# Windowed attention with keys on the partitions: four heads a step, maxima taken apart, keys projected between two groups of queries

## The reference, cut to what matters

```
q  = rope(h @ w_q)                       # 512 x 16 x 64; k, v: 512 x 2 x 64, shared by 8 heads each
sc = einsum(q, [k of the tile before, k of this tile]) * 64 ** -0.5
sc = where(0 <= query - key < 128, sc, NEG)           # 4 tiles of 128 queries, 128 or 256 keys
mx = maximum(sc.max(-1), sink)
e  = exp(sc - mx)
p  = e / (e.sum(-1) + exp(sink - mx))
return (p @ v) @ w_out                                 # 1024 x 1024
```

## Time and profile before

| | us |
|---|---|
| median of 3 runs (lowest to highest) | 2175.12 (2169.94 to 2177.8) |
| the profiled execution: its own time | 2168.92 |
| its span in the profile | 2167.1 |
| PE busy | 2060.9 (95%) |
| DVE busy | 1450.6 (67%) |
| ACT busy | 976.3 (45%) |
| granted TensorE clock, mean of the run | 0.982 |

### The profile page before, as it was taken

How to read it: one execution, slowest core, us unless ns; L and a number is a source line. 1 busy time by engine, 2 the same in 40 slices (tenths; PEclk the granted TensorE clock), 3 DMA queues, 4 the chain that set the end, 5 groups by cost and what they waited for, 6 DMA issues and landing times.

```text
span 2167.1 us, 29621 instructions
## 1 busy us (share of the span) xinstructions
PE 2060.9 (95%) x9716; PEld 1653.1 (76%) x9716; DVE 1450.6 (67%) x2421; ACT 976.3 (45%) x1625; POOL 11.1 (1%) x25
## 2 busy tenths in 40 slices
PE   5989999997999989999999999999999999999997
PEld 5988888876777667766667788888877777888885
DVE  6885434463899965667765788883377758888633
ACT  3345433452777632546664433333236743333321
POOL 0000000001000000000000000000000000000000
PEclk9999999987999999999999999999999999999999
DMA  4220122321999705420001233223340022332332
GB/s 153 88 69 1 49 92 92 97 78 39 334 354 358 254 30 155 117 59 1 1 1 50 88 97 97 89 95 107 107 126 25 0 78 87 97 97 90 99 105 84
DMA packets 65175, 218.97 MB, mean 101 GB/s; under 512 B 9392, under 2 KB 10544, under 8 KB 64960
## 3 DMA queue, kind: packets, MB, share of 16 engines
q1 hardware_dynamic: 59792, 210.73, 29.3%
q10 hardware_dynamic: 5296, 7.12, 1.3%
HBM read 209.03 MB, written 2.10 MB: 97 GB/s over the span
## 4 chain that ended last, share of the span: by engine, by line
PE 80%; DVE 12%; ACT 3%; issue 3%; DMA 1%; ACTq 1%; DVEq 0%; SPq 0%
PE psum L812 53%; PE psum L1202 5%; PE psum L1375 2%; PE psum L935 2%; DVE sig L2439 2%; PE psum L958 2%; DVE w_lo L2174 2%; PE psum L975 2%; PE psum L1143 1%; PE psum L974 1%; PE psum L1175 1%; PE psum L1185 1%; PE psum L1358 1%; PE psum L1311 1%; PE psum L931 1%
## 5 line engine op out<-in xcount | busy, mean ns | idle before, releaser
L812 PE MATMUL psum<-x_hi,w_hi 128*128 128x512 f32 (+1 forms) x1440 | 514.5, 375 | 17.8 <-DVE x_lo L2208 6.6
L812 PE MATMUL psum<-x_lo,w_hi 128*128 128x512 f32 (+1 forms) x1440 | 514.0, 374 | 0.0
L812 PE MATMUL psum<-x_hi,w_lo 128*128 128x512 f32 (+1 forms) x1440 | 511.2, 372 | 0.0
L2174 DVE TENSOR_TENSOR w_lo<-raw,w_hi 128x1024 fp32r<-128x1024 f32 x243 | 295.8, 1221 | 198.9 <-ACT w_hi L1498 198.3
L1498 ACT ACTIVATE w_hi<-raw 128x1024 fp32r<-128x1024 f32 x243 | 255.1, 1053 | 184.8 <-DMA raw<-stream 184.5
L812 PEld LDWEIGHTS psum<-x_hi,w_hi 128*128 128x128 f32 x1440 | 263.4, 190 | 73.2 <-issue 8.3
L812 PEld LDWEIGHTS psum<-x_lo,w_hi 128*128 128x128 f32 x1440 | 262.6, 190 | 50.1 <-issue 1.0
L812 PEld LDWEIGHTS psum<-x_hi,w_lo 128*128 128x128 f32 x1440 | 262.8, 190 | 48.6
L812 PE MATMUL psum<-hid_hi,w_hi 128*128 128x512 f32 x624 | 244.4, 392 | 3.4 <-DVE hid_lo L3032 2.0
L812 PE MATMUL psum<-hid_lo,w_hi 128*128 128x512 f32 x624 | 244.7, 392 | 0.0
L812 PE MATMUL psum<-hid_hi,w_lo 128*128 128x512 f32 x624 | 244.0, 391 | 0.0
(11 more groups left out here) (537 smaller groups left out, 3188.7 us busy)
## 6 DMA issues: line engine op xcount, KB each, us to landing
raw<-stream SPq DMA_DIRECT2D x251, 512.0 KB, 3.5
raw<-experts SPq DMA_DIRECT2D x70, 512.0 KB, 5.2
raw_more<-experts SPq DMA_DIRECT2D x68, 512.0 KB, 5.4
staged<-staged ACTq DMA_DIRECT2D x84, 64.0 KB, 2.9
resid<-x_fm SPq DMA_DIRECT2D x4, 528.0 KB, 7.3
out_fm<-resid SPq DMA_DIRECT2D x4, 512.0 KB, 2.9
consts<-consts_in SPq DMA_DIRECT2D x1, 1373.0 KB, 14.2
kv_pairs<-kv_even_odd ACTq DMA_DIRECT2D x4, 256.0 KB, 4.0
```

Of the source, the lines that this page charges most:

```text
L812: last = pe.matmul(o, wt[:, slot, k * P:(k + 1) * P], m[part], start=start and p == 0, stop=stop and p == 2, skip_group_check=True)
L2174: dve.tensor_tensor(w_lo[:, slot, :], raw[:, slot, :], w_hi[:, slot, :].bitcast(F32), ALU.subtract)\
```

## The change

- **Order of the stream.** Queries in two groups of four units, q3a and q3b, with k3 and v3 between them: q3a, k3, v3, q3b, wo3. The inputs of keys and values are made two chunks in each of the four rounds of q3a, by one operation of ACT (L2318) and one of DVE (`kv_low`, L3314).
- **Forms.** Each rotated chunk of queries is written twice, as high part (ACT, `window_queries_high`) and low part (DVE, `window_queries_low`, L3339), stacked on the partitions, in `window_q_parts`; the keys likewise (`window_keys_hi_twice`, `window_keys_lo_and_max`). `window_q_and_max` holds the high part of the queries, and in one row below it the negative maximum.
- **Maxima.** 64 products of high parts (L1563), in 32 fills of two tiles each, alternate in the PSUM banks 1 and 3. DVE reads each fill with two operations that add the band and keep the maximum (L3371). Sixteen fills stand between the units of q3b, four behind each; two stand before the first step and fourteen between the steps of the first quad. A quad is four chunks, eight heads. The maxima of a quad are turned (L1574), joined with the sinks, negated by ACT (L2386) and moved into rows by two DMAs of ACT (L2391).
- **Steps.** Two quads of 14 steps each; a step is (query tile, group, own keys or those before) for four heads: three float32r products of 512 columns (L1589 to L1591: stacked score, mask, stacked score with maximum), one exponential of 512 (L2412), and two steps later one float32 product of 512 columns with the values beside ones (L1603). The sums come out of it as a row.
- **Sums.** SP moves them to rows by DMA, DVE adds the sink's term and takes reciprocals of 32 rows in stretches of 384 and 128 columns. They are split, spread over the partitions by two products (L1613), and DVE weighs the outputs. Per quad this comes after its last step; the first quad's lies beside the second quad's steps.
- **Output projection.** The first four units of wo3 take chunks 0 to 3 (the first quad) each, with the second quad's four spreads behind the second unit, and then chunks 4 to 7, one chunk for each of the four units in turn. So all four slots of weights are held until chunk 7. Units 4 to 7 are as before.

```diff
-         ("q3", 8), ("k3", 1), ("v3", 1), ("wo3", 8), ("ffn1_in", 2 * FC), ("ffn1_out", 24)]
+         ("q3a", 4), ("k3", 1), ("v3", 1), ("q3b", 4), ("wo3", 8), ("ffn1_in", 2 * FC), ("ffn1_out", 24)]
...
+            def window_maxima(f):
+                p, g, first = f // W_FILLS, f // 2 % B_G, 2 * (f % 2)
+                pe.wait_ge(qw_ready, 2 * p + g + 1)
+                if f == 0:
+                    pe.wait_ge(kw_hi, 1)
+                if f >= 2:
+                    pe.wait_ge(wmax_read, 2 * f - 2)
+                for t in (first, first + 1):
+                    k0 = P * max(t - 1, 0)
+                    mm = pe.matmul(window_max_bank(f)[:, 2 * P * (t - first):2 * P * (t - first) + P * (t + 1) - k0], window_parts(g, p)[:, window_tile(t)],
+                                   KW1[:, g, k0:P * (t + 1)], start=True, stop=True)
+                mm.then_inc(wmax_done, 1)
...
+            def window_scores(q, i):
+                t, g, back = W_STEPS[i]
+                n, j = N_W * q + i, t - back
+                if i == 0:
+                    pe.wait_ge(qmw_hi, W_FILLS * (q + 1))
+                    pe.wait_ge(wmax_rows[q], 16 * B_G)
+                if n >= 2:
+                    pe.wait_ge(wexp_done, n - 1)
+                s = by_head(window_score_bank(n))
+                pe.matmul(s, KW1[:, g, window_tile(j)], QW[q][g][:, :, window_tile(t)], start=True, stop=False, skip_group_check=True)
+                pe.matmul(s, (BANDW if back else CAUW)[:, :], ID4[:, :, :], start=False, stop=False, skip_group_check=True)
+                pe.matmul(s, KW2[:, g, window_tile(j)], QMW[q][g][:, :, window_tile(t)], start=False, stop=True, skip_group_check=True).then_inc(ws_done, 1)
+            def window_outputs(q, i):
+                t, g, back = W_STEPS[i]
+                n, x = N_W * q + i, 2 * QT * q + 2 * t + g
+                pe.wait_ge(wexp_done, n + 1)
+                first = back == 1 or t == 0
+                if first and x >= 2:
+                    pe.wait_ge(wo_kept, x - 1)
+                pe.matmul(window_out_bank(x), VW[:, t - back, g * HD:g * HD + P], PW[:, n % 4, :], start=first, stop=back == 0, skip_group_check=True)\
+                  .then_inc(wpv_done, 1)
...
+            for c in range(QUAD, 2 * QUAD):
+                n, r = U["q3b"] + c - QUAD, later_result(c)
+                unit(n, n % SLOTS, r, r % PAIRS, T2, x_of(T2))
+                if c == QUAD:
+                    pe.wait_ge(scaled, 12)
+                    turn(r + 1, VFM[:, :], T2)
+                for f in range(W_FILLS * (c - QUAD), W_FILLS * (c - QUAD + 1)):
+                    window_maxima(f)
+            turn_window_maxima(0)
+            for f in range(W_FILLS * QUAD, W_FILLS * QUAD + 2):
+                window_maxima(f)
...
+            for q in range(QUADS):
+                for i in range(N_W):
+                    window_scores(q, i)
+                    if q == 0:
+                        for f in range(W_FILLS * QUAD + 2 + 2 * i, min(W_FILLS * QUAD + 4 + 2 * i, 2 * W_FILLS * QUAD)):
+                            window_maxima(f)
+                        if i == N_W - 3:
+                            turn_window_maxima(1)
+                    elif 7 <= i < 7 + QUAD:
+                        spread_window(i - 7)
+                    if i >= 2:
+                        window_outputs(q, i - 2)
+                    elif q:
+                        window_outputs(q - 1, N_W + i - 2)
...
+            for c in range(LATE):
+                late_window_chunks(c, range(0, QUAD))
+                if c == 1:
+                    for p in range(QUAD, 2 * QUAD):
+                        spread_window(p)
+            for k in range(QUAD, C):
+                for c in range(LATE):
+                    late_window_chunks(c, range(k, k + 1))
...
+            def rope_unit(n, r, e, turn, scale):
+                by_unit(n)
+                stage(r % PAIRS, e, e % EV_SLOTS, T2, back=2, scale=scale)
+                high_weights(n + AHEAD)
+                swap_halves(e, turn, r + 1)
...
+            for c in range(QUAD, 2 * QUAD):
+                low_weights(U["q3b"] + c - QUAD + AHEAD)
+                rope_turned(c + 1, later_result(c), E0["q3b"] + 2 * (c - QUAD), TURN0["q3b"] + c - QUAD)
+                if c > QUAD:
+                    window_queries_low(c - 1)
+                for f in range(W_FILLS * (c - QUAD), W_FILLS * (c - QUAD + 1)):
+                    read_window_maxima(f)
+            sinks_in_maxima(0)
...
-            rotated("q3", U["q3"], 8, lambda c: Q3[:, c, :], COSR[:, :], SINR[:, :], kv_input)
...
-            attention("swa")
-            residual("wo3", T2, "nf_1", "ffn1")
```

569 lines of the change are left out of this document (411 added, 158 removed).

## The result

The changed kernel takes 2189.96 us (median of 5 runs, 2186.97 to 2191.71) against 2175.12: 14.8 us more, ratio 1.0069 (95% interval 1.0053 to 1.0085). The forecast was 2194, slower, with +18.9 us.

What follows compares the result with a forecast made beforehand. PE, busy 2060.9 of 2167.1 us, was taken to set the time. Three stretches, +55.1 - 48.3 + 12.1 = +18.9 us, on the median of 2175.12 gave 2194; range 2176 to 2206.

Steps and rivals of the forecast that it cites:

- stretch 1: From q3a's start to the first attention step: 118.7 us against 63.6, +55.1.
- stretch 2: Attention: 57.0 us against 105.3, -48.3.
- stretch 3: Output projection (wo3): 56.8 us against 44.7, +12.1; bounds +6 to +15.
- The loop: In q3b, fills wait for DVE reads queued behind the rotation; PE idles, next unit runs cold: three loops of 18.3 us.
- first gap: PE's idle time behind the first unit of q3b, waiting for rotation, reads and last fill: 8.8 us.
- the sign: What would show the forecast right: PE idle before L1563 for around 10 us, DVE named, four times in q3b.
- Keys and values: In k3, PE waits 5.0 us for input chunk 6, made late by DVE's rounds in q3a.
- Attention: 28 steps of 0.70 + 0.91 us, with fills, transposes, spreads 1.9, waits and a cold start: 57.0 us.
- Rival D: Attention's steps are set by the PE-ACT hand-over; at 2.1 us a step +14, total 2205; 8%.
- Output projection: wo3: 44.7 us of units, spreads 1.9, late shares 1.9, a 5.75 wait for weights, cold start 2.5.
- Rival B: The loop holds but waits don't cost the clock; six cold starts (14.8 us) go, leaving +4: 2179; 13%.
- Rival C: The q3b loop doesn't bind; DVE's 7.4 us a unit paces it, 10.9 less each: -14, 2161; 9%.

Runs made afterwards that it cites:

- e1: Changed kernel with only DVE's order altered: in each q3b round the four fills are read before the low weights and rotation; 2160.56 us, ratio to before 0.9923.
- all five moves: Changed kernel plus maxima reads before the rotation, four maxima banks, reordered late wo3 chunks, constant forms later and POOL's clearing later; 2155.31 us, ratio to before 0.9911.
- seven moves: Kernel with all five moves, plus key/value inputs made 3, 3, 2, 0 and first quad's sinks, turning and negation ahead of the last rotation; 2151.44 us.
- the late chunks alone: Changed kernel with only wo3's late chunks reordered: units 0 to 2 in turn, unit 3's four as a block behind them; 2187.49 us.
- the forms later: Changed kernel with the six constant-form copies behind q3a's last low part and POOL's first clearing one unit later; 2188.10 us.
- four banks: Changed kernel with the maxima fills in four PSUM banks (1, 3, 5, 7) instead of two, DVE's order untouched; 2165.02 us, ratio to before 0.9935.
- the fills ahead: Kernel with seven moves, plus the sixteen fills placed 5, 5, 6, 0 behind q3b's four units; 2154.16 us, ratio to before 0.9904.

## Why the prediction held, and where its terms were off

The sum was +18.9 and the stage took +15.7 norm to norm (+14.8 in medians). By its own three stretches, cut from the first matmul of q3a as there (1575.09 in the profile after):

| | forecast | measured |
|---|---|---|
| stretch 1 | +55.1 | +53.5 |
| stretch 2 | -48.3 | -51.0 |
| stretch 3 | +12.1 | +14.3 |

These add up to 16.7 and not to the ruler's 15.7, because they begin at q3a's first matmul, a microsecond of the change ahead of the first sum.

- **The loop.** Forecast: first gap 8.8, then three loops of 18.3. Measured: 9.2 (1624.35 to 1633.55), and 18.25, 16.90, 17.47. Two experiments that open it in different ways take 29 and 25 us off; the mechanism is shown. PE's waits at L1563 were 6.0 to 8.8 us, not the 10 that was named as the sign, and the mean granted clock fell from 0.982 to 0.969 as named. The loop's length was a little large for two reasons. The unit behind a wait was put at 8.1 and took 7.42, 6.86 and 6.96 (5.59 at full clock): half clock costs 1.3 to 1.8 us, not 2.5. And the sine started 4.1 to 4.9 us behind the first DMA's issue, not 4.6 to 5.2.
- **Keys and values.** 5.0 forecast, 1.23 + 4.28 measured.
- **Attention.** 57.0 forecast, 54.2 measured. The step was right: 1.555 us (product with the values 0.86, the three others 0.70) against 1.61. The waits inside were overrated: between the quads 1.44 us with no releaser shown, and no other wait over 0.3 us in that stretch. The first quad's spreads were underrated: a step with one takes 2.41 us, 0.86 more, so 3.4 for the four and not 1.9. Rival D is out.
- **Output projection.** Gap 5.46 (5.75 forecast), wait for the shares 2.25 (1.9), spreads 2.10 (1.9). The 5.75 rests on a slip: 1173.21 to 1180.79 is 7.58 and not 7.85, and no row gives the other 0.27. With 7.58 the gap would have been 5.48. The missing 2 us: there are two starts at half clock, behind the spreads' wait as well, and I had counted one.
- **Rival B** (no clock cost) is wrong in the rows and in the run with PE kept busy. The 14.8 that it was given, six starts at 2.3 to 2.5, is near the truth by two errors: a start cost less, but PE ran at half clock in more places, in the fills, the turning and the spreads too. In stretches of half a microsecond, PE's busy time multiplied by what the granted clock lacks to 1.00 adds up to 13.7 us between the two sums (8.7, 1.6 and 3.4 in the three stretches), an estimate. **Rival C** (the loop doesn't bind) would have been true with one list written in another order: e1 lies at 2160.6, and C was worked out at 2161. That closeness is partly luck, as C took rounds of 7.4 us and e1's are 8.0.
- The Trainium skill's rule in "DMA: Bandwidth & Descriptors", "Rules for kernel authors" (issue early, wait late) pointed the right way. The run without the DMAs gives it a size: 7.0 of some 30 us. By the fixed cost of 2.0 us that the same page of the Trainium skill gives for GpSimd's DMAs ("Anatomy of one DMA — SWDGE (gpsimd) path") the forecast would have been +14, an estimate. The profile's page of the changed kernel shows 3.2 us from issue to landing for ACT's, so that is no support for it, though the total lies near.
- Errors partly cancel: the first two stretches came out 1.6 and 2.7 us below the forecast and the third 2.2 above. The total is nearer than its parts, and that much is luck.

What stays open: the kernels with five and with seven moves came out 3 to 8 us above what was expected. DVE's pace in q3b is 1.7 of it in the first: from the end of q3b's first unit to the first step it took 35.7 us where 34 was expected. The rows show the wait that moved to v and the longer half clock in the last stretch beside it; why the clock stayed low for longer there, no run shows.

## What to carry to other kernels

When a producer's buffers are freed by a consumer that has other duties, look at where the freeing stands in the consumer's list: a read of 1.4 us that stands behind a rotation, a DMA and two low parts costs PE all of them, each round. Write the freeing first; or give it so many buffers that it may be a round late; either took back 25 to 29 us here for a few lines. And after each such move read the lists of all engines again, since the item moved past (the weights, the negation) is the next one that somebody waits for, as two of these experiments had to find out.

## What the runs showed of the hardware that was not expected

**POOL's clearing stops one kind of DVE operation.** In the changed kernel POOL clears 128x2048 twice as q3a starts. POOL's and DVE's timelines:

```profile
1575.56 3.56 POOL L887 MEMSET window_q_and_max<- 128x2048 f32 x2
```

```profile
1576.53 0.69 DVE L2548 TENSOR_TENSOR squares<-squares 128x512 f32<-128x512 f32 x1
1577.13 2.27 DVE L2565 TENSOR_SCALAR scratch<-resid,vecs 128x512 f32<-128x512 f32 x1
```

The operation with two tensors takes its usual 0.69 beside the clearing; the one with a tensor and scalars takes 2.27 and ends at 1579.40, just behind the clearing's end at 1579.12. The other 31 of its kind have a median of 0.48. With the clearing one unit later all 32 take 0.48 to 0.49, and PE's wait of 0.70 before the norm sum is gone. The Trainium skill, "SBUF — State Buffer", "SBUF: two separate sides", says that DVE in a mode with two ports and GpSimd take a shared pair of ports by an exclusive lock, and that DVE with two inputs is blocked only by a GpSimd operation that reads. A clearing does not read: its row names no input. The rows agree with the half on two inputs, and with the other one if the operation that was held runs in such a mode, which no row tells.

**The clock does not follow one wait alone.** In the run with PE kept busy, the stretches 1646 and 1662 are alike in every column, with idle times of 1.18 and 1.21 us ahead of them. Behind the first the clock stayed at 1.00, behind the second it was 0.50 from 1665 for some three microseconds. The wait of 2.25 us for the shares shows it more strongly. It is the same in every kernel that has the spreads behind the second unit, with the same matmuls on both sides. In the changed kernel it ends at 1754.85, and the clock is at half from 1756.9 to 1760.3:

```profile
1756.00:1757.00 1.00, 1.00 (x6) 0.56 (x4) 0.97 (x2) 0.00 (x0) 0.00 (x0) 0.95 0.00 0
...
1760.00:1761.00 1.00, 1.00 (x5) 0.85 (x4) 0.97 (x2) 0.36 (x1) 0.00 (x0) 0.85 0.00 0
```

In the kernel with all five moves it ends at 1715.71, and the clock is at half from 1716.5 to 1723.3, twice as long:

```profile
1716.00:1717.00 1.00, 1.00 (x5) 0.77 (x5) 0.53 (x1) 0.00 (x0) 0.00 (x0) 0.74 0.00 0
...
1723.00:1724.00 1.00, 1.00 (x5) 0.77 (x5) 0.97 (x2) 0.34 (x1) 0.00 (x0) 0.84 0.00 0
```

Reads first, the late chunks alone and the forms later have it as short as the changed kernel; four banks, the run without the DMAs, seven moves and the fills ahead have it long; and in the run with PE kept busy the clock stays at 1.00 behind the same wait. One can't tell from a single wait of this kernel whether it will cost the clock, or for how long.

**Work outside the change drifts.** The start of the first norm sum varies from 1575.2 to 1590.6 in the profiles of kernels that are alike up to q3a, more than most effects in the stage. A ruler inside the stage was needed to read a difference of 2 us.
